# Rotary transfers behind the index copies, half a gate tile ahead of the sample's heads, gate halves regrouped behind the scans

## What is computed

```
h = rmsnorm(x); P = h @ w_in            # columns: rwkv, sparse attention, retention, gates
y_rw  = rwkv_mixer(P_rw)                # token shift, LoRA, chunked scan with a 64x64 state per head
y_sa  = dsa_mixer(P_sa)                 # rotary q, k, index q, index k; index scores; top-k; attention
y_ret = retention_mixer(P_ret)          # four heads, chunks of 64
x = x + (sum of sigmoid(P_gate) * (y @ w_branch)) @ w_o
x = x + relu(rmsnorm(x) @ w_up)**2 @ w_down
```

## Time and profile before

| what | value |
| --- | --- |
| median of 3 runs | 2665.7 us (2663.76 to 2669.13) |
| profiled execution, its own time | 2665.5 us |
| its span, first to last instruction | 2663.5 us |
| PE busy | 2547.8 us, 96% |
| DVE busy | 1207.8 us, 45% |
| ACT busy | 579.3 us, 22% |
| POOL busy | 1327.5 us, 50% |
| mean granted clock of PE | 0.982 |

### The profile page before, as it was taken

How to read it: one execution, slowest core, us unless ns; L and a number is a source line. 1 busy time by engine, 2 the same in 40 slices (tenths; PEclk the granted TensorE clock), 3 DMA queues, 4 the chain that set the end, 5 groups by cost and what they waited for, 6 DMA issues and landing times.

```text
span 2663.5 us, 62404 instructions
## 1 busy us (share of the span) xinstructions
PE 2547.8 (96%) x24614; PEld 2378.9 (89%) x24614; DVE 1207.8 (45%) x2244; ACT 579.3 (22%) x1147; POOL 1327.5 (50%) x1780
## 2 busy tenths in 40 slices
PE   7997999999989999999999889998999899999998
PEld 7986887799969999999999868877999799999998
DVE  5354886554455421121343558855444553221224
ACT  3121222412123211011220212223221322110112
POOL 6633543322226766666775334433112277666665
PEclk9998999999999999999999989999999999999999
DMA  5212112211135222222242211122111342222221
GB/s 193 96 48 68 57 56 71 109 48 48 44 121 171 89 87 80 87 79 87 79 150 66 72 50 64 52 76 108 44 40 52 142 161 80 88 80 87 82 83 67
DMA packets 67754, 223.84 MB, mean 84 GB/s; under 512 B 8769, under 2 KB 9665, under 8 KB 66497
## 3 DMA queue, kind: packets, MB, share of 16 engines
q1 hardware_dynamic: 45360, 160.46, 17.8%
q10 hardware_dynamic: 22160, 60.03, 6.7%
HBM read 190.25 MB, written 29.03 MB: 82 GB/s over the span
## 4 chain that ended last, share of the span: by engine, by line
PE 91%; DVE 2%; ACT 2%; ACTq 2%; issue 1%; DVEq 1%; POOL 0%; DMA 0%; POOLq 0%
PE dense L539 75%; PE mix L539 15%; DVEq L1554 1%; PE mix L958 1%; ACT region_b L1076 1%; ACTq L1143 1%; ACTq L1144 1%; ACT x L1076 1%; POOL w_lo L526 0%; PE dense L958 0%; ACT in_hi L1076 0%; DVE act_lo L1572 0%; DVE region_b L2037 0%; DVE x L2126 0%; DVE region_b L2035 0%
## 5 line engine op out<-in xcount | busy, mean ns | idle before, releaser
L522 POOL TENSOR_SCALAR w_hi<-w_raw 128x512 fp32r<-128x512 f32 x592 | 372.7, 647 | 1290.7 <-PE dense L539 995.3
L526 POOL TENSOR_TENSOR w_lo<-w_raw,w_hi 128x256 fp32r<-128x256 f32 x1184 | 954.8, 836 | 24.7
L539 PE MATMUL dense<-act_hi,w_hi 128*128 128x288 f32 x2272 | 693.0, 316 | 28.6 <-POOL w_lo L526 12.4
L539 PE MATMUL dense<-in_hi,w_hi 128*128 128x288 f32 x2432 | 678.7, 294 | 9.8 <-DVE in_lo L2053 8.7
L539 PE MATMUL dense<-in_lo,w_hi 128*128 128x288 f32 x2432 | 678.4, 295 | 0.0
L539 PE MATMUL dense<-act_lo,w_hi 128*128 128x288 f32 x2272 | 656.5, 300 | 2.0 <-issue 2.0
L539 PE MATMUL dense<-act_hi,w_lo 128*128 128x288 f32 x2272 | 540.5, 299 | 0.0
L539 PE MATMUL dense<-in_hi,w_lo 128*128 128x288 f32 x2432 | 522.2, 296 | 0.0
L539 PEld LDWEIGHTS dense<-act_hi,w_hi 128*128 128x128 f32 x2272 | 437.5, 193 | 88.8 <-issue 58.2
L539 PEld LDWEIGHTS dense<-in_hi,w_hi 128*128 128x128 f32 x2432 | 458.4, 189 | 10.9 <-DVE in_lo L2053 8.9
L539 PEld LDWEIGHTS dense<-in_lo,w_hi 128*128 128x128 f32 x2432 | 458.7, 189 | 0.0
(11 more groups left out here) (200 smaller groups left out, 2544.5 us busy)
## 6 DMA issues: line engine op xcount, KB each, us to landing
w_raw<-in_stream SPq DMA_DIRECT2D x296, 512.0 KB, 3.2
y_mix<-gate_scratch ACTq DMA_DIRECT2D x48, 288.0 KB, 3.2
gate_scratch<-region_b ACTq DMA_DIRECT2D x36, 288.0 KB, 2.3
x_scratch<-x ACTq DMA_DIRECT2D x2, 2304.0 KB, 12.3
y_scratch<-y_mix ACTq DMA_DIRECT2D x2, 2304.0 KB, 7.3
x<-x_scratch ACTq DMA_DIRECT2D x2, 2304.0 KB, 9.9
y_mix<-y_scratch ACTq DMA_DIRECT2D x2, 2304.0 KB, 9.1
gate_scratch<-region_a ACTq DMA_DIRECT2D x12, 288.0 KB, 2.1
```

The costliest lines, as they stand in the source:

```text
L522: hi = nc.gpsimd.tensor_scalar(w_hi[:, v, c], w_raw[:, s, c], 1.0, 1.0, ALU.mult, ALU.mult)
L526: lo = nc.gpsimd.tensor_tensor(w_lo[:, v, c], w_raw[:, s, c], w_hi[:, v, c].bitcast(F32), ALU.subtract)
L539: return nc.tensor.matmul(out, lhsT, rhs, start=start, stop=stop, skip_group_check=True)
```

## The change

1. `away` only copies and frees; the swap DMAs are a step of their own, `swap`. On ACT's queue it stands behind `out(1)` of retention (t = 0), behind `rs0` (t = 1), behind `rs2` (t = 2), where it was (t = 4), and behind the tile's Relus (t = 5 to 8), followed there by `old_keys`. For t = 2 two of the four DMAs go (only 64 rows are used).
2. DVE's order: the first `logits(0, 0)` stands ahead of the rotary step n = 14 instead of behind it; the rotary step n = 15 moves from ahead of the heads into run 0, behind its `logits`. `prob_t` gets its place behind `prob` in the buffer.
3. `MID_FILL` gets a first step of 4 slices, done by PE at the end of run 31, behind `scores(4, 0)` and `scores(4, 1)`. All steps move on by one; the bodies' share falls from 96 to 92 slices.
4. In the preparation, DVE's `gates_beside` calls are regrouped: two halves behind the third scan (j = 2), one behind the fourth, one behind the second norm and one behind the fourth, none between the stage and the first body. ACT's list `ended` is one step deep instead of two.

```diff
-MID_FILL = SAMPLE_FILL * 8 + PREP_FILL
+MID_FILL = (4,) + SAMPLE_FILL * 8 + PREP_FILL
...
                         if run == 31:
...
                                 scores(4, h)
-
-                beside = iter(range(16, len(MID_FILL)))
+                            fill_halves(l, mid_range(0))
+
+                beside = iter(range(17, len(MID_FILL)))
...
                     if i == 1:
                         away(l, 0)
                     out(i)
+                    if i == 1:
+                        swap(l, 0)
                 away(l, 1)
...
+            def swap(l, t):
+                n = SA_STEP[t]
                 if n == 8:
                     act.wait_ge(rope_zero, l + 1)
-                for r in (0, C):
+                for r in (0, C) if n != 10 else (0,):
                     act.dma_start(s_trot[r:r + 8, n % 2, :], s_raw[r + 8:r + 16, n % 2, :]).then_inc(rope_swapped[n % 2], 16)
                     act.dma_start(s_trot[r + 8:r + 16, n % 2, :], s_raw[r:r + 8, n % 2, :]).then_inc(rope_swapped[n % 2], 16)
...
                     (post_sq if name.startswith("sq") else post_rs)(int(name[-1]))
+                    if name == "rs0":
+                        swap(l, 1)
                     if name == "rs1":
                         away(l, 2)
+                    if name == "rs2":
+                        swap(l, 2)
...
                         away(l, t)
-                        old_keys(t)
+                        if t == 4:
+                            swap(l, t)
+                            old_keys(t)
...
                             if t == N_SA - 1 and i == 0:
                                 exps(0, 0)
+                        swap(l, t)
+                        old_keys(t)
...
-                for n in range(8, 16):
+                for n in range(8, 15):
...
+                    if n == 14:
+                        logits(0, 0)
                     rope(l, n, s_raw, s_tcos, s_trot, s_cos, s_sin, dst, rows)
...
                     if n == 14:
-                        logits(0, 0)
                         index(4)
...
+                        if run == 0:
+                            rope(l, 15, s_raw, s_tcos, s_trot, s_cos, s_sin, ysa[:, 3, :])
+                            settle()
...
-                gates_beside(ended, 16)
+                gates_beside(ended, 17)
...
-                    if j < 3:
-                        gates_beside(ended, 17 + j)
+                    if j == 2:
+                        gates_beside(ended, 18, 19, 20, 21)
+                        gates_beside(ended, 22)
+                    if j == 3:
+                        gates_beside(ended, 23)
...
-                    gates_beside(ended, 20 + j)
+                    if j % 2:
+                        gates_beside(ended, *{1: (24,), 3: (25,)}[j])
...
                 rwkv_stage(l, 0)
-                gates_beside(ended, 24)
```

More of the change, by code:

```diff
@@ L300, in build @@
         top8 = cs(8)
-        prob_t = cs(2, 512)
         stat = cs(2, 4)
@@ L314, in build @@
         logit, prob = cs(2, T), cs(2, T)
+        prob_t = cs(2, 512)
         cs_end = cs.at
@@ L965, in _ @@
                         else:
-                            fill_halves(l, mid_range(2 * h))
+                            fill_halves(l, mid_range(2 * h + 1))
                         pe.wait_ge(at_turned_sb, l * 40 + (run + 1))
@@ L978, in _ @@
                         else:
-                            fill_halves(l, mid_range(2 * h + 1))
+                            fill_halves(l, mid_range(2 * h + 2))
                         if run == 31:
@@ L1432, in _ @@
                         if b == 4:
-                            away_beside(ended, 2 * h)
-                            away_beside(ended, 2 * h + 1)
+                            for step in ((0, 1, 2) if h == 0 else (2 * h + 1, 2 * h + 2)):
+                                away_beside(ended, step)
                             ahead(run)
@@ L1443, in _ @@
                 act.dma_start(y_dram, y_mix[:, :, :]).then_inc(y_away, 16)
-                ended = [ended[0] + ended[1], ended[2] + ended[3]]
+                ended = [sum(ended, [])]
                 act.wait_ge(lw_clear, l + 1)
@@ L1456, in _ @@
                         op(a_b[:, j, :], ps[:, 0:TX], ACT.Sigmoid, bias=pr("a0", j)).then_inc(lora_act.sem, 1)
-                        away_beside(ended, 16 + j)
+                        away_beside(ended, 17 + j)
                 nc.scalar.preload_act_table_set(EXP_LN)
@@ L1463, in _ @@
                     op(clamped[:, j, :], clamped[:, j, :], ACT.Exp, scale=-0.5, bias=small[:, 2:3]).then_inc(lora_act.sem, 1)
-                for step in (20, 21):
+                for step in (21, 22):
                     away_beside(ended, step)
@@ L1468, in _ @@
                 rwkv_stage(l, 0)
-                for step in (22, 23, 24):
+                for step in (23, 24, 25):
                     away_beside(ended, step)
@@ L1585, in residual, with swapped_by @@
                     low_part(n, m, hi, lo, gain)
+            def swapped_by(l, n):
+                return l * (256 - 32 * (n % 2 == 0)) + 64 * ((n - 8) // 2 + 1) - 32 * (n % 2 == 0 and n >= 10)
             def rope(l, n, raw, tc, tr, cos, sin, dst, rows=P):
@@ L1591, in rope @@
                 if n >= 8:
-                    dve.wait_ge(rope_swapped[n % 2], l * 256 + 64 * ((n - 8) // 2 + 1))
+                    dve.wait_ge(rope_swapped[n % 2], swapped_by(l, n))
                     passed()
@@ L1969, in _ @@
                         if b == 4:
-                            gates_beside(ended, 2 * h, 2 * h + 1)
+                            gates_beside(ended, *((0, 1, 2) if h == 0 else (2 * h + 1, 2 * h + 2)))
                         if run == 35:
```

## The result

| | us |
|---|---|
| before, median of 4 runs | 2667.4 |
| changed, median of 4 runs | 2643.9 |
| ratio, 95% interval | 0.9916, 0.990 to 0.993 |
| profiled execution after: time, span | 2640.55, 2638.4 |

What follows compares the result with a forecast made beforehand. TensorE, busy 96% of the span, was taken as the bound, losing time to holes and low clock. Terms -38.2 - 5.2 - 8.4 + 0 = -51.8 against 2665.5 gave 2614 us, range 2602 to 2637.

Steps and rivals of the forecast that it cites:

- Index stage, holes and clock: Index stage: Relus ahead of DMAs save 14.5 us of TensorE holes a layer, and 6.3 and 7.5 us of clock.
- Rival (c): Whole change: the holes are VectorE's after all and saved Relu waits reappear elsewhere; 2664 to 2667 us; chance 0.03.
- Cached keys: End of index stage: key loads issued 7 to 8 us behind tile 7 arrive late, 0.5 us a layer.
- Rival (a): Index stage: VectorE's chain takes over through longer products, ending at the last scores; 9 us in all, 2623; chance 0.2.
- Rotary step 15: Attention heads: moved into VectorE's first head, it makes TensorE wait 1.8 us a layer in the second head.
- rival (d): Attention heads: VectorE becomes the bound, each of 31 heads in two layers waits 0.9 us; 2670 us; chance 0.03.
- Retention and post-norm: Retention and post-norm: moved swaps unblock ACT's results, -2.6 us a layer (bounds -2.2 and -4.2), sum -5.2.
- Half a tile: Ahead of the sample's heads: four slices fill TensorE's hole; -3.3 wait, -1.3 clock, +0.4 bodies a layer, -8.4 in all.
- Gate halves: Preparation of the scan: second of two TensorE waits goes; VectorE's chain -0.7, clock +1.3, sum 0 (bounds -3, +5).
- Rival (b): Index stage: the clock stays low because the work is thin, not because of holes; 2630 us; chance 0.15.

Runs made afterwards that it cites:

- run 1: Not a follow-up kernel: the pass of the second attention head within the kernel, where TensorE waits for VectorE's scaling; 3.0 us a layer in the changed kernel.
- run 32: Not a follow-up kernel: the pass of the sample's first head within the kernel, right after the half tile's four slices; TensorE waited 3.6 us a layer there before.
- the three mends: The changed kernel with early key loads, top-k rounds taken out of the first head and the gate part undone: 2604.8 us, ratio to before 0.9780.

## Why the prediction was wrong

- **Index stage, holes and clock: right.** With the keys out of the way the stage took 41.2 and 41.3 us in the two layers, which the sum had at 41.5 (61.83 - 14.5 - 6.3 + 0.5) and 41.6. The wait for the Relus fell by 14.3 us a layer (33.8 to 5.3), against a term of 14.5, so the clock term of 6.3 to 7.5 us was about right too. Rival (c), that the holes are DVE's, is out with it.
- **Cached keys: the first step that failed.** "I add 0.5 us a layer (bounds 0 and 2)." It was 3.3 us of wait, and 3.3 to 6.2 of clock behind it, which stood in no term. By the runs with and without it, 17.7 us for both layers. I had let the Relus of tile 7 end 4 us behind the tile. They ended 7.7 us behind, because the third one waits for the index sum and this for a rotary step. The sum had this step end 1.7 us behind tile 7; it ended 5.2 us behind (224.08). The top-k rounds ahead of it ended 1.5 us behind the tile and not 0.7 us ahead of it, and the step took 3.5 us (1.11, 1.27, 1.14), not 2.3. I had written of heads 0 and 1, which don't need VectorE, and hung the loads behind heads 2 and 3, which do.
- **Rival (a)** had a part of this mechanism, VectorE's longer products, but not the path: the chain doesn't end at the last scores, it ends in ACT's queue, at loads that have nothing to do with VectorE. Its price of 9 us was half of what it cost.
- **Rotary step 15: right place, 1.2 us short.** 2.96 us in place of 1.8: the step took 3.4 us (248.13 to 251.51), not 2.3. And the clock behind this new hole, 1.6 us between the second head and the third (6.81 us in place of 5.24), was again not in the sum. Between the third head and head 31 nothing is lost, 166.6 us against 166.4 before: "it catches up at once" holds, and rival (d) is out.
- **Retention and post-norm: low in layer 0, near in layer 1.** 4.8 us are gained by the end of tile 5 in layer 0 and about 2 in layer 1 (16.0 at that point, of which 14.0 come from layer 0); 2.6 a layer stood in the sum, 4.2 was its outer bound. No run takes this part alone.
- **Half a tile: right sign, too small.** 8.4 forecast, about 13 by the traces. The wait for the first probabilities of the sample is gone, and the earlier trace rows's slow stretch with it: ahead of and in run 32 PE is at 1.00.
- **Gate halves: the second step that failed.** "-0.7 DVE chain, +1.3 clock: 0", bounds up to +5; by the traces it was +15, by the times 17. The step from two waits of PE to one was wrong: the half tile alone had already taken the second wait, and the first grew from 1.14 to 3.31 us and stayed. The DVE chain came out at +2.6 us a layer, not -0.7 (from the last head to the first body 43.8 us, 41.2 before): I had counted the removed wait of 1.66 us and not the one that takes its place, 2.17 us. ACT's late table load and the half more ahead of the stage I had put at 1.0 us together. And I read the edit of ACT's list (`ended` from two steps to one) as bookkeeping: it makes each store wait for a half that VectorE has still to take, in the bodies too, where I had no term.
- **Rival (b)**, the clock doesn't come back: no, with the keys early the stage is granted 1.00 up to the first head. It stays low where a hole was left.

In sum: of 28 us missing, the three mends give back 39, so with them the change is worth about 60 us (2666.0 - 2604.8), more than the 52 of the sum: the half tile and layer 0 of the retention gave more than their terms, for no reason that the forecast names.

## What to carry to other kernels

When an instruction is moved behind another on an in-order queue, go on through everything that is queued behind both: here four DMAs were moved behind a Relu that waits for VectorE, and two unrelated loads went with them. Loads that depend on nothing belong ahead of anything that can wait. Every hole left on TensorE should be priced with the clock behind it, which here cost one to three times the hole again; and where two waits lie beside each other, taking one away shows nothing, so try both together before calling either harmless. Where a change has several parts, price each part with the others in place: here one part had already removed the wait that another was made for.

## What the runs showed of the hardware

The price of a hole isn't its length. 1.55 us without work on TensorE was followed by 17.0 us at a mean of 0.70, 3.25 us by 15.25 us at 0.78, and a like hole in another execution of the same code by 18.15 us at 0.64, where 11.9 us at 1.00 is the full-speed length. The clock came back each time while TensorE worked on, some 8 us behind the hole in the changed kernel and 12 to 13 us behind it in the other two, so an edit that halves a hole can measure as nothing.

VectorE's products have two lengths here as in the earlier trace rows, and now the other engine can be named. With the gate part undone, GpSimd stands idle up to 510.83, and the five products of 128x577 before it take 0.75 to 0.76 us; the three behind it 1.01, 0.79 and 1.14:

```profile
510.48 0.75 DVE L2028 TENSOR_TENSOR region_a<-region_a,x 128x577 f32<-128x577 f32 x1
510.83 1.96 POOL L522 TENSOR_SCALAR w_hi<-w_raw 128x512 fp32r<-128x512 f32 x2 [8.11 <-PE dense L539]
511.30 1.01 DVE L2030 TENSOR_TENSOR region_b<-region_a,region_b 128x577 f32<-128x577 f32 x1
```

In the changed kernel GpSimd starts at 508.04, and all eight products from 508.25 on take 0.92 to 1.30 us, 8.7 us against 6.7. This agrees with the rule of the Trainium skill (SBUF — State Buffer, Who interferes with whom) that a VectorE instruction with two SBUF inputs and a GpSimd instruction that reads SBUF exclude each other. It also lets the costs of the change feed on each other: counted from the last head, the products start 2.8 us later in the changed kernel and GpSimd's splits 1.1 us earlier, and so they meet. No run here moves GpSimd's splits alone.
